# Weight rings kept across two stage borders, with the first two tiles split in the stage ahead

## The chip, the cores and the metric

The kernel runs on one core of a Trainium2 chip. Its engines are TensorE (PE; weight loads stand as PEld), VectorE (DVE), ScalarE (ACT), GpSimd (POOL) and SyncE (SP), which here only issues transfers. The metric is device time in microseconds of one execution; lower is better.

## The reference

Two layers of a diffusion backbone over 512 latent tokens and 256 context tokens of width 1024, all in float32. Each layer does, in this order for what matters here:

```python
P = _in_proj(h, w_in)                     # q, k, v, f, cs, co, gate: h @ w_in, column groups
cs = _token_shift(P['cs'], mu)            # inputs of the RWKV-7 branch
o_a = diff. attention(q, k, v)            # with 2-D rotary
o_f = real(fftn(f))                       # Fourier mixing over tokens and 128-wide groups
o_c = RWKV-7 scan in both directions      # state 64x64 per head, 8 heads
g = sigmoid(gate)
y = g0 * (o_a @ w_pa) + g1 * (o_f @ w_pf) + g2 * (o_c @ w_pc)
x = LN(alpha * x + gate1 * (y @ w_o))     # then a ConvGLU feed-forward sublayer of the same form
```

In the last layer only the latent tokens go through attention, the merges and the feed-forward part.

## The kernel before, in words

A layer is a row of stages. Each is a `with stage(nc)` block in which the five engines run their own instruction lists and meet through semaphores; at its end all engines meet, and the next stage begins with new semaphores. In order: `rwkv_inputs` (norm, then the projection of the `cs` and `co` columns, N = 15 tiles of 128 columns), `rwkv_scan`, `attention`, `merge_pa` (o_a @ w_pa, 8 tiles, with the RWKV output's group norm beside it), `close` (w_pc, w_pf, w_o and the Fourier transform), `ffn`.

**Weight tiles.** All big products are float32 made of three passes, (hi, hi), (hi, lo) and (lo, hi): each weight tile of 1024 x 128 is loaded into a ring `w_raw`, ACT copies it to the high part (`split_hi`, L324, counted by `w_hi`), and POOL subtracts that from the raw tile to get the low part (`split_lo`, L330, counted by `w_lo`). PE waits for `w_lo` before it uses a tile and counts `w_used` behind it. `weight_rings(sc, n_raw, n_split)` allocates the three rings. Before the change each stage allocates its own: 3 raw and 2 split buffers in `rwkv_inputs`, `rwkv_scan` and `close`, 2 and 2 in `merge_pa`. So the first tile of a stage is loaded and split after the stage has begun. `load_weights` (L313 to L316) makes SP wait until the buffer's last tile is split.

**The scan.** `rwkv_scan` works through six groups of 128 tokens, in both directions at once. Its many small matmuls wait for DVE and ACT, and PE fills these waits with the projection of the other `w_in` columns (v, f, gates, q, k): the `slots`, one weight tile each. `fill(point, g)` (L844 to L861) puts the next parts at named points of a group; `fill("first", 0)` runs the first 8 parts, tiles 0 and 1 and the latent half of tile 2, ahead of everything else. A tile has a piece of 512 latent tokens and one of 256 context tokens; the pieces use PSUM banks 6 and 7 in turn, so piece i waits at `result` for ACT's copy of piece i - 2 (L850, L1062). On ACT these copies stand in program order behind `decays(0, 0)` and `decays(0, 1)` (L1099, L1100), the exponentials (L1087 to L1097) of the cumulative sums that DVE makes in `sums` (L1148 to L1163); between the two, DVE does `scaled(0, 0)` (L1170 to L1184). `sums(0, d)` needs the inputs `sg`, `a`, `k`, `kk` of direction d, which SP loads in `inputs(0)` behind two mask tables and the load of tile 0; the rope table and tiles 1 and 2 follow. For tiles 0 and 1 POOL also makes the high part (L811), for later ones ACT does it once the copies of tile s - 2 are made (L1072 to L1081).

**The merge and `close`.** In `merge_pa` SP's loads are interleaved with `gate_in`, which waits for DVE's gated product (L1700) of tile j - 2. DVE's last product is the end of the stage, after PE's last tile. `close` starts with SP's loads of w_pc tiles 0 and 1 (512 rows, so half tiles of 256 KB), then the Fourier inputs `f`, the table `dft_w`, a gate and the big DFT tables. ACT copies the four parts of `oc` to `oc_hi` with the splits of the first two tiles between them (L1898, L1895), DVE makes `oc_lo` (L1993), PE multiplies tile 0 by k, and after every second k does one step of the transform (L1827), the first of which needs `f` and `dft_w`.

The lines the prediction speaks of:

```python
pe.wait_ge(sem("w_lo"), s + 1)                 # L848, the filler tile's low part
if i >= 2:
    pe.wait_ge(sem("result"), i - 1)           # L850, the bank of piece i - 2 is copied out
...
decays(0, 0)                                   # L1099, ACT, ahead of all copies
decays(0, 1)
copy_pieces(0, "first")
```

## Time and profile before

| | us |
|---|---|
| median of 3 runs | 3865.76 (3857.37 to 3866.92) |
| profiled execution: its own time | 3858.9 |
| its span | 3857.1 |
| mean granted TensorE clock | 0.957 |
| PE busy | 3435.0 (89%) |
| DVE, ACT, POOL busy | 1570.8 (41%), 1295.1 (34%), 1146.3 (30%) |
| DMA queue q1 | 413.55 MB, 33.9% of 16 engines |
| load of a w_in tile, 512 KB | 5.6 to landing, median |

Times in the trace count from the start of the span. The scan of layer 0 begins at 253.8, that of layer 1 at 2383.5; `close` begins at 1345.2 and 3283.6. "Idle before" in a row is how long the engine did nothing until that instruction, with what released it last. A granted clock of 1.00 is TensorE's upper level (2.4 GHz), 0.50 the lower one (1.2 GHz).

### The profile page before, as it was taken

The numbers are of one execution on the slowest core, as the hardware profiler recorded it, in microseconds if no ns is written. First come the engines' busy times: TensorE is split into PE (matmuls) and PEld (weight loads), VectorE is DVE, ScalarE is ACT, GpSimd is POOL, SyncE is SP. The second block draws the span as 40 slices with busy tenths as digits, with TensorE's granted clock in tenths as the row PEclk, the third lists the DMA queues.
The fourth block names the chain that finished last, engine by engine and source line by source line (L and its number), as shares of the span: only waits on it lengthen the run. The fifth ranks groups of instructions, "written<-read, shape, count | busy, mean of one in ns | idle before, by whom it ended". The sixth has DMA issues, their size and how long they took to land. (4 is left out here: it accounts for less than half of the span.)

```text
span 3857.1 us, 82372 instructions
## 1 busy us (share of the span) xinstructions
PE 3435.0 (89%) x36724; PEld 2751.4 (71%) x36724; DVE 1570.8 (41%) x2337; ACT 1295.1 (34%) x2096; POOL 1146.3 (30%) x677
## 2 busy tenths in 40 slices
PE   5979999999887899599999697999999897869997
PEld 3658888888655677487878465888878565558886
DVE  3243334432377544612121534344443375362224
ACT  3322233333255422321212243333433365233222
POOL 2111132233001512433323332213333104245554
PEclk9989999999998999799999898999999998989998
DMA  6653323442222342133332145333342214423332
GB/s 223 225 183 107 109 88 92 121 124 91 76 73 73 121 143 89 50 117 120 114 126 82 44 134 165 102 106 120 118 119 87 94 66 125 166 71 93 94 98 87
DMA packets 444250, 427.60 MB, mean 111 GB/s; under 512 B 15540, under 2 KB 369002, under 8 KB 436986
## 3 DMA queue, kind: packets, MB, share of 16 engines
q1 hardware_dynamic: 442314, 413.55, 33.9%
q10 hardware_dynamic: 1584, 8.78, 0.6%
q8 instruction: 290, 4.75, 0.5%
q14 instruction: 62, 0.51, 0.0%
HBM read 333.54 MB, written 88.74 MB: 109 GB/s over the span
## 5 line engine op out<-in xcount | busy, mean ns | idle before, releaser
L856 PE MATMUL ps<-I-280_h_hi,I-1958_w_hi 128*128 128x256 f32 (+1 forms) x832 | 299.4, 360 | 19.1 <-POOL I-1959_w_lo L330 19.0
L856 PE MATMUL ps<-I-281_h_lo,I-1958_w_hi 128*128 128x256 f32 (+1 forms) x832 | 283.3, 340 | 3.4 <-issue 3.4
L856 PE MATMUL ps<-I-280_h_hi,I-1959_w_lo 128*128 128x256 f32 (+1 forms) x832 | 283.1, 340 | 0.0
L2223 POOL TENSOR_TENSOR I-18452_w_lo<-I-18450_w_raw,I-18451_w_hi 128x1024 fp32r<-128x1024 f32 x65 | 156.9, 2414 | 374.6 <-ACT I-18451_w_hi L2182 374.5
L856 PE MATMUL ps<-I-23226_h_hi,I-24623_w_hi 128*128 128x512 f32 (+1 forms) x544 | 214.4, 394 | 17.4 <-POOL I-24624_w_lo L330 15.6
L2223 POOL TENSOR_TENSOR I-38403_w_lo<-I-38401_w_raw,I-38402_w_hi 128x1024 fp32r<-128x1024 f32 x65 | 156.3, 2405 | 168.3 <-ACT I-38402_w_hi L2182 168.3
L856 PE MATMUL ps<-I-23226_h_hi,I-24624_w_lo 128*128 128x512 f32 (+1 forms) x544 | 201.9, 371 | 0.0
L856 PE MATMUL ps<-I-23227_h_lo,I-24623_w_hi 128*128 128x512 f32 (+1 forms) x544 | 201.6, 371 | 0.0
L2182 ACT ACTIVATE I-18451_w_hi<-I-18450_w_raw 128x1024 fp32r<-128x1024 f32 x65 | 68.9, 1060 | 386.7 <-PE ps L339 236.4
L330 POOL TENSOR_TENSOR I-1959_w_lo<-I-1957_w_raw,I-1958_w_hi 128x1024 fp32r<-128x1024 f32 x36 | 88.4, 2455 | 334.3 <-ACT I-1958_w_hi L1080 334.1
L856 PEld LDWEIGHTS ps<-I-280_h_hi,I-1958_w_hi 128*128 128x128 f32 x832 | 157.9, 190 | 41.5 <-POOL I-1959_w_lo L330 19.9
L339 PE MATMUL ps<-I-18447_h_hi,I-18451_w_hi 128*128 128x512 f32 x704 | 185.2, 344 | 1.0 <-DVE I-18448_h_lo L381 1.0
L339 PE MATMUL ps<-I-18447_h_hi,I-18452_w_lo 128*128 128x512 f32 x704 | 181.5, 339 | 0.0
L339 PE MATMUL ps<-I-18448_h_lo,I-18451_w_hi 128*128 128x512 f32 x704 | 180.7, 338 | 0.0
L330 POOL TENSOR_TENSOR I-24624_w_lo<-I-24622_w_raw,I-24623_w_hi 128x1024 fp32r<-128x1024 f32 x36 | 90.3, 2508 | 283.4 <-ACT I-24623_w_hi L1080 283.2
L856 PEld LDWEIGHTS ps<-I-280_h_hi,I-1959_w_lo 128*128 128x128 f32 x832 | 158.1, 190 | 22.7 <-issue 3.8
L856 PEld LDWEIGHTS ps<-I-281_h_lo,I-1958_w_hi 128*128 128x128 f32 x832 | 158.4, 190 | 14.4
L1062 ACT ACTIVATE I-1960_result<-ps 128x512 f32<-128x512 f32 x104 | 51.2, 493 | 342.1 <-PE ps L856 342.0
L339 PE MATMUL ps<-I-38398_h_hi,I-38402_w_hi 128*128 128x512 f32 x352 | 137.6, 391 | 1.9 <-DVE I-38399_h_lo L381 1.9
L2182 ACT ACTIVATE I-38402_w_hi<-I-38401_w_raw 128x1024 fp32r<-128x1024 f32 x65 | 68.9, 1060 | 205.7 <-PE ps L339 119.6
L339 PE MATMUL ps<-I-38398_h_hi,I-38403_w_lo 128*128 128x512 f32 x352 | 136.9, 389 | 0.0
L339 PE MATMUL ps<-I-38399_h_lo,I-38402_w_hi 128*128 128x512 f32 x352 | 136.9, 389 | 0.0
(856 smaller groups left out, 8922.7 us busy)
## 6 DMA issues: line engine op xcount, KB each, us to landing
I-1957_w_raw<-in_w_in SPq DMA_DIRECT2D x52, 512.0 KB, 5.6
I-24622_w_raw<-in_w_in SPq DMA_DIRECT2D x52, 512.0 KB, 5.3
I-18460_ada_w<-in_ada_w SPq DMA_DIRECT2D x24, 1024.0 KB, 5.9
I-18450_w_raw<-in_ffn_up SPq DMA_DIRECT2D x44, 512.0 KB, 3.9
I-38401_w_raw<-in_ffn_up SPq DMA_DIRECT2D x44, 512.0 KB, 3.9
proj_d<-I-1960_result SPq DMA_DIRECT2D x52, 384.0 KB, 2.8
I-482_ada_w<-in_ada_w SPq DMA_DIRECT2D x16, 1024.0 KB, 5.7
I-18450_w_raw<-in_ffn_down SPq DMA_DIRECT2D x22, 512.0 KB, 3.3
```

Of the source, the lines that this page charges most:

```text
L330: eng.tensor_tensor(rings[2][:, n % n_split, 0:kt, :], rings[0][:, n % n_raw, 0:kt, :], rings[1][:, n % n_split, 0:kt, :].bitcast(F32), AL ...
L339: m = pe.matmul(dst[:, at:at + n], w[wi][:, k, :], a[ai][:, k, at:at + n], start=k == 0 and i == 0, stop=k == kt - 1 and i == 2)
L856: m = pe.matmul(bank(6 + i % 2, n_c), w[:, k, :], hv[:, k, c0:c0 + n_c], start=k == 0 and v == 0, stop=k == KT - 1 and v == 2)
L1062: act.activation(res[:, s % 2, c0:c0 + n_c], bank(6 + i % 2, n_c), ACT.Copy, scale=DH_A ** -0.5 if J_Q <= slots[s][0] < J_K else 1.0).then ...
L2182: act.activation(rings[1][:, g % 2, :, :], rings[0][:, g % 3, :, :], ACT.Copy).then_inc(sem("w_hi"), 1)
L2223: pool.tensor_tensor(rings[2][:, g % 2, :, :], rings[0][:, g % 3, :, :], rings[1][:, g % 2, :, :].bitcast(F32), ALU.subtract).then_inc(sem ...
```

## The change

The rings of `rwkv_inputs` and `rwkv_scan` become one set, allocated ahead of both, and so do those of `attention` (which only takes the argument), `merge_pa` and `close`, with 3 raw and 2 split buffers.

`rwkv_inputs` loads three more tiles at the end (numbers 15, 16 and 17 of its ring, which are slots 0, 1 and 2 of the scan) and splits the first two: ACT's split of tile 15 stands ahead of its work for main tile 14, that of tile 16 behind it. SP issues the three loads right after the loop, ahead of the last ada load and of the last stores, and waits for the third before the stage ends. The scan starts with slots 0 and 1 split and slot 2 loaded; its ring positions are shifted by 15 (`o_w`), and its semaphores count from slot 2 for `w_hi` and `w_lo` and from slot 3 for the loads. The loads of slots 0 to 2, POOL's copies and splits of slots 0 and 1, and ACT's wait for `w_lo` before it makes a high part are gone.

`merge_pa` loads the first two tiles of w_pc as its tiles 8 and 9 and splits both: tile 8 before ACT's sigmoid for j = 7, tile 9 as ACT's last instruction, since it needs the buffer of tile 7. POOL's splits stand around `out(3)`. `close` starts with its tile 2.

```diff
@@ -485,6 +484,9 @@
                     sp.dma_start(raw_d[:, R_G, 0:width(R_G)], gd[:, 0:width(R_G)]).then_inc(sem("raw_out"), 16)
                 if n >= 13:
                     store_lora(n - 9)
+            for n in range(N, N + 3):
+                c = OFF_V + (n - N) * P
+                load_weights(sp, sem, rings, n, src[:, :, c:c + P])
             if ada:
                 ada_load(sp, sem, ring, N, ada[N])
...
@@ -583,8 +586,7 @@
                     act.activation(inv[:, :], side[0:HC, :], ACT.Sqrt).then_inc(sem("norm"), 1)
 
             for n in range(N):
-                if n + 1 < N:
-                    split_hi(act, sem, rings, n + 1)
+                split_hi(act, sem, rings, n + 1)
                 beside(2 * n)
+            split_hi(act, sem, rings, N + 1)
...
-            for n in range(1, N):
+            for n in range(1, N + 2):
                 split_lo(pool, sem, rings, n)
...
-    rings = weight_rings(s2, 3, 2)
+    raw = lambda s: rings[0][:, (s + o_w) % 3]
+    hi, lo = (lambda s, i=i: rings[i][:, (s + o_w) % 2] for i in (1, 2))
...
-                load_weights(sp, sem, rings, s, w_src[:, :, c:c + P])
+                if s >= 5:
+                    sp.wait_ge(sem("w_lo"), s - 4)
+                sp.dma_start(raw(s), w_src[:, :, c:c + P]).then_inc(sem(f"w_in{s % 3}"), 16)
...
             sp.dma_start(masks[:, :, :], A["masks"]).then_inc(sem("const"), 16)
             sp.dma_start(lvm[:, :, :], A["lvmasks"]).then_inc(sem("const"), 16)
-            load(0)
             inputs(0)
             sp.dma_start(rope[:, :, :], A["rope"]).then_inc(sem("rope"), 16)
-            load(1)
-            load(2)
...
-                if s < 2:
-                    pool.wait_ge(sem(f"w_in{s % 3}"), 16 * (s // 3 + 1))
-                    pool.tensor_copy(rings[1][:, s % 2, :, :], rings[0][:, s % 3, :, :]).then_inc(sem("w_hi"), 1)
+                pool.wait_ge(sem("w_hi"), s - 1)
                 if s in turned:
...
-                    split_lo(pool, sem, rings, s)
+                    pool.tensor_tensor(lo(s), raw(s), hi(s).bitcast(F32), ALU.subtract).then_inc(sem("w_lo"), 1)
...
-            split(0)
-            split(1)
             for s in range(2, len(slots)):
                 pool.wait_ge(sem("piece"), ends[s - 2])
                 split(s)
...
                     if ks[0] == 0:
-                        pe.wait_ge(sem("w_lo"), s + 1)
+                        if s >= 2:
+                            pe.wait_ge(sem("w_lo"), s - 1)
                         if i >= 2:
                             pe.wait_ge(sem("result"), i - 1)
...
                             if i + 1 == ends[s] and s + 2 < len(slots):
-                                act.wait_ge(sem("w_lo"), s + 2)
-                                act.wait_ge(sem(f"w_in{(s + 2) % 3}"), 16 * ((s + 2) // 3 + 1))
-                                w_in, w_out = rings[0][:, (s + 2) % 3], rings[1][:, s % 2]
+                                if s >= 1:
+                                    act.wait_ge(sem(f"w_in{(s + 2) % 3}"), 16 * ((s + 2) // 3))
+                                w_in, w_out = raw(s + 2), hi(s + 2)
...
-        rings = weight_rings(sc, 2, 2)
...
+        after = A["w_pc"][l].rearrange("(k p) n -> p k n", p=P)
...
+            for j in range(2):
+                load_weights(sp, sem, rings, KT + j, after[:, :, j * P:(j + 1) * P])
...
             for j in range(KT):
-                if j + 1 < KT:
-                    split_hi(act, sem, rings, j + 1)
+                split_hi(act, sem, rings, j + 1, HA if j + 1 < KT else CTILES)
...
+            split_hi(act, sem, rings, KT + 1, CTILES)
...
+            split_lo(pool, sem, rings, KT, CTILES)
             out(3)
-
-def close(l, oc, y, last):
+            split_lo(pool, sem, rings, KT + 1, CTILES)
...
-        rings = weight_rings(s2, 3, 2)
+        raw = lambda n: rings[0][:, (n + KT) % 3]
+        hi, lo = (lambda n, i=i: rings[i][:, (n + KT) % 2] for i in (1, 2))
...
-                if n >= 3:
-                    sp.wait_ge(sem("w_lo"), n - 2)
+                if n >= 5:
+                    sp.wait_ge(sem("w_lo"), n - 4)
                 if n < M:
                     kind, j = slots[n]
-                    sp.dma_start(rings[0][:, n % 3, 0:CTILES, :], w_in[kind][:, :, j * P:(j + 1) * P]).then_inc(sem(f"w_in{n % 3}"), 16)
+                    sp.dma_start(raw(n)[:, 0:CTILES, :], w_in[kind][:, :, j * P:(j + 1) * P]).then_inc(sem(f"w_in{n % 3}"), 16)
...
-            weights(0)
-            weights(1)
             sp.dma_start(f[:, :, 0:n_tok], proj_d[J_F:J_F + F_GROUPS, :, 0:n_tok].rearrange("j p n -> p j n")).then_inc(sem("f"), 16)
             sp.dma_start(dw[:, :], A["dft_w"]).then_inc(sem("f"), 16)
             gate_in(0)
...
-                whi, wlo = slot(rings, n)
-                pe.wait_ge(sem("w_lo"), n + 1)
+                whi, wlo = hi(n), lo(n)
+                if n >= 2:
+                    pe.wait_ge(sem("w_lo"), n - 1)
...
-                act.wait_ge(sem(f"w_in{n % 3}"), 16 * (n // 3 + 1))
-                if n >= 2:
-                    act.wait_ge(sem("w_used"), n - 1)
-                act.activation(rings[1][:, n % 2, 0:kt_of(n), :], rings[0][:, n % 3, 0:kt_of(n), :], ACT.Copy).then_inc(sem("w_hi"), 1)
+                act.wait_ge(sem(f"w_in{n % 3}"), 16 * (n // 3 + (n % 3 == 2)))
+                act.wait_ge(sem("w_used"), n - 1)
+                act.activation(hi(n)[:, 0:kt_of(n), :], raw(n)[:, 0:kt_of(n), :], ACT.Copy).then_inc(sem("w_hi"), 1)
 
             for k in range(CTILES):
                 act.activation(ocp[0][:, k, :], oc[:, k, 0:n_tok], ACT.Copy).then_inc(sem("oc_hi"), 1)
-                if k < 2:
-                    split(k)
...
-            for n in range(N):
-                split_lo(pool, sem, rings, n, kt_of(n))
+            for n in range(2, N):
+                pool.wait_ge(sem("w_hi"), n - 1)
+                pool.tensor_tensor(lo(n)[:, 0:kt_of(n), :], raw(n)[:, 0:kt_of(n), :], hi(n)[:, 0:kt_of(n), :].bitcast(F32),
+                                   ALU.subtract).then_inc(sem("w_lo"), 1)
...
-            rwkv_inputs(l, h, last)
+            rings = weight_rings(s2, 3, 2)
+            n_w = rwkv_inputs(l, h, rings, last)
             with ExitStack() as s3:
-                rwkv_scan(l, s3, h, last)
+                rwkv_scan(l, s3, h, rings, n_w, last)
         oc = sb(sc, "oc", [P, CTILES, TOK])
         y = sb(sc, "y", [P, KT, TOK])
+        rings = weight_rings(sc, 3, 2)
         with ExitStack() as s2:
             oa = x[:, :, :].rearrange("p t d -> p (t d)").rearrange("p (j n) -> p j n", j=HA)
-            attention(l, oa, last)
-            merge_pa(l, oa, oc, y, last)
-        close(l, oc, y, last)
+            attention(l, oa, rings, last)
+            merge_pa(l, oa, oc, y, rings, last)
+        close(l, oc, y, rings, last)
```

## Rows read from the trace of the kernel before

**Rows 1.** The page's costliest groups: line, engine, shapes, count | busy, mean ns | idle before, releaser.

```profile
L856 PE MATMUL ps<-I-280_h_hi,I-1958_w_hi 128*128 128x256 f32 (+1 forms) x832 | 299.4, 360 | 19.1 <-POOL I-1959_w_lo L330 19.0
...
L330 POOL TENSOR_TENSOR I-1959_w_lo<-I-1957_w_raw,I-1958_w_hi 128x1024 fp32r<-128x1024 f32 x36 | 88.4, 2455 | 334.3 <-ACT I-1958_w_hi L1080 334.1
```

**Rows 2.** Timeline of PE, scan of layer 0: start us, us, engine, line [idle before].

```profile
264.77 0.79 PE L856 MATMUL ps<-I-280_h_hi,I-1958_w_hi 128*128 128x512 f32 x1 [15.45 <-POOL I-1959_w_lo L330]
...
275.50 0.28 PE L856 MATMUL ps<-I-280_h_hi,I-1959_w_lo 128*128 128x256 f32 x1
279.28 0.50 PE L856 MATMUL ps<-I-280_h_hi,I-1958_w_hi 128*128 128x512 f32 x1 [3.50 <-POOL I-1959_w_lo L330]
...
289.37 0.39 PE L856 MATMUL ps<-I-280_h_hi,I-1958_w_hi 128*128 128x512 f32 x1
```

**Rows 3.** Timeline of PE, scan of layer 1.

```profile
2394.58 0.80 PE L856 MATMUL ps<-I-23226_h_hi,I-24623_w_hi 128*128 128x512 f32 x1 [15.56 <-POOL I-24624_w_lo L330]
...
2407.49 0.47 PE L856 MATMUL ps<-I-23226_h_hi,I-24623_w_hi 128*128 128x512 f32 x1 [1.84 <-ACT I-24625_result L1062]
...
2415.91 0.28 PE L856 MATMUL ps<-I-23226_h_hi,I-24624_w_lo 128*128 128x256 f32 x1
```

**Rows 4.** Timeline of SP's queue, start of the scan, layer 0.

```profile
254.66 0.43 SPq L316 DMA_DIRECT2D I-1957_w_raw<-in_w_in  x1
```

**Rows 5.** Timelines of DVE, then POOL, then ACT, scan of layer 0.

```profile
261.36 1.23 DVE L1148 TENSOR_TENSOR_SCAN I-1943_L<-I-1914_reset,I-1931_sg 128x512 f32<-128x512 f32 x1 [6.74 <-DMA I-1931_sg<-sg_d]
262.62 2.65 DVE L1150 TENSOR_TENSOR I-1944_Lx<-I-1943_L,I-1931_sg 128x512 f32<-128x512 f32 x1
...
272.42 1.23 DVE L1148 TENSOR_TENSOR_SCAN I-1943_L<-I-1914_reset,I-1932_sg 128x512 f32<-128x512 f32 x1
...
261.55 3.17 POOL L330 TENSOR_TENSOR I-1959_w_lo<-I-1957_w_raw,I-1958_w_hi 128x1024 fp32r<-128x1024 f32 x1
...
275.01 0.63 ACT L1087 ACTIVATE I-1944_Lx<-I-1944_Lx 128x512 f32<-128x512 f32 x1 [6.58 <-DVE I-1934_Lr L1153]
...
277.56 0.87 ACT L1062 ACTIVATE I-1960_result<-ps 128x512 f32<-128x512 f32 x2
```

**Rows 6.** Timeline of DVE, scan of layer 1.

```profile
2392.42 2.65 DVE L1150 TENSOR_TENSOR I-24609_Lx<-I-24608_L,I-24596_sg 128x512 f32<-128x512 f32 x1
...
2402.76 1.53 DVE L1153 TENSOR_TENSOR I-24599_Lr<-I-24608_L 128x512 f32<-128x512 f32 x1
```

**Rows 7.** Timelines around merge and close, layer 0: DVE, SP, ACT, PE, POOL.

```profile
1343.37 0.95 DVE L1700 TENSOR_TENSOR I-13482_y<-I-16057_gate,ps 128x768 f32<-128x768 f32 x1 [7.36 <-PE ps L339]
...
1345.22 0.94 SPq L1785 DMA_DIRECT2D I-16885_w_raw<-in_w_pc  x2
...
1348.05 0.63 ACT L1895 ACTIVATE I-16886_w_hi<-I-16885_w_raw 128x512 fp32r<-128x512 f32 x1 [1.98 <-DMA I-16885_w_raw<-in_w_pc]
...
1350.09 1.01 PE L339 MATMUL ps<-I-16900_oc_hi,I-16886_w_hi 128*128 128x512 f32 x2 [6.76 <-POOL I-16887_w_lo L330]
...
1355.33 2.07 PE L1827 MATMUL ps<-I-16902_dft_w,I-49_x 128*128 128x256 f32 x4 [1.03 <-DMA I-16902_dft_w<-in_dft_w]
...
1360.98 1.29 POOL L330 TENSOR_TENSOR I-16887_w_lo<-I-16885_w_raw,I-16886_w_hi 128x512 fp32r<-128x512 f32 x1 [8.98 <-ACT I-16886_w_hi L1895]
```

**Rows 8.** Windows: stretch, length, busy (count) per engine, PE clock, DMA share, GB/s.

```profile
256.00:261.00 5.00, 0.00 (x0) 0.00 (x0) 0.00 (x0) 0.00 (x0) 0.57 (x1) 0.50 1.05 302
264.80:269.90 5.10, 5.10 (x12) 4.03 (x13) 4.96 (x9) 2.50 (x6) 0.00 (x0) 0.50 1.13 298
1346.50:1350.00 3.50, 0.00 (x0) 0.00 (x0) 1.12 (x2) 1.95 (x4) 1.24 (x1) 0.79 0.89 275
...
2376.00:2394.00 18.00, 2.90 (x4) 1.16 (x4) 4.36 (x5) 1.28 (x1) 4.23 (x3) 0.50 0.84 261
```

**Rows 9.** Timeline of DVE, end of the merge, layer 1.

```profile
3282.04 0.69 DVE L1700 TENSOR_TENSOR I-34669_y<-I-36620_gate,ps 128x512 f32<-128x512 f32 x1 [4.75 <-PE ps L339]
```

**Rows 10.** One line's instructions, L619: ns min/median/max, first and last start.

```profile
L619 DVE SCALAR_TENSOR_TENSOR I-283_k_and_kk<-I-283_k_and_kk,I-53_pa,ps x4: 1004/1010/1015, 230.2 to 249.4; 128x768 f32<-128x768 f32 x4
```

More of the change, by code:

```diff
@@ L419, in program, with rwkv_inputs @@
         LAT = ((0, SEQ),)
-        def rwkv_inputs(l, h, last):
+        def rwkv_inputs(l, h, rings, last):
             mains = (R_W, R_A, 0, 1, 2, 3, R_G, 10, 11, 12, 13, 4, 5, 6, 7)
@@ L503, in _ @@
                     sp.wait_ge(sem("kept"), 16)
+                    sp.wait_ge(sem(f"w_in{(N + 2) % 3}"), 16 * ((N + 2) // 3 + 1))
                 @block.tensor
@@ L648, in _, with rwkv_scan @@
                         ada_add(dve, sem, 1, 0, 2, 7)
-        def rwkv_scan(l, s2, h, last):
+            return N
+        def rwkv_scan(l, s2, h, rings, o_w, last):
             G = [P, GCOL]
@@ L808, in split @@
                     def split(s):
[L809 to L811 removed]
+                        pool.wait_ge(sem("w_hi"), s - 1)
                         if s in turned:
[L813 removed]
                             for v in range(2):
[L815 to L816 removed]
+                                m = pool.tensor_tensor(halves(lo(s))[:, :, v], paired(raw(s))[:, :, v],
+                                                       halves(hi(s))[:, :, v].bitcast(F32), ALU.subtract)
                             m.then_inc(sem("w_lo"), 1)
                         else:
[L819 removed]
+                            pool.tensor_tensor(lo(s), raw(s), hi(s).bitcast(F32), ALU.subtract).then_inc(sem("w_lo"), 1)
                     def rotate(s):
@@ L1276, in _, with attention @@
                                 dve.tensor_tensor(y, y, half(2 * d).rearrange("p i (t c) -> p t i c", t=CTILES), ALU.add).then_inc(sem("Ysum"), 1)
-        def attention(l, oa, last):
+        def attention(l, oa, rings, last):
             nq = LT if last else NT
@@ L1516, in _, with merge_pa @@
                             act.activation(oa[:, j, 0:q_tok], p_of(j), ACT.Copy, scale=subln[l][:, :]).then_inc(sem("oa"), 1)
-        def merge_pa(l, oa, oc, y, last):
+        def merge_pa(l, oa, oc, y, rings, last):
             seqs = LAT if last else BOTH
@@ L1728, in _, with close @@
                             out(j - 3)
+                    split_lo(pool, sem, rings, KT, CTILES)
                     out(3)
-        def close(l, oc, y, last):
+                    split_lo(pool, sem, rings, KT + 1, CTILES)
+        def close(l, oc, y, rings, last):
             seqs = LAT if last else BOTH
@@ L1780, in weights @@
                     def weights(n):
-                        if n >= 3:
-                            sp.wait_ge(sem("w_lo"), n - 2)
+                        if n >= 5:
+                            sp.wait_ge(sem("w_lo"), n - 4)
                         if n < M:
                             kind, j = slots[n]
-                            sp.dma_start(rings[0][:, n % 3, 0:CTILES, :], w_in[kind][:, :, j * P:(j + 1) * P]).then_inc(sem(f"w_in{n % 3}"), 16)
+                            sp.dma_start(raw(n)[:, 0:CTILES, :], w_in[kind][:, :, j * P:(j + 1) * P]).then_inc(sem(f"w_in{n % 3}"), 16)
                         else:
                             _, c, k = slots[n]
-                            sp.dma_start(wide(rings[0][:, n % 3]), w_o[:, 2 * k:2 * k + 2, c * 512:(c + 1) * 512]).then_inc(sem(f"w_in{n % 3}"), 16)
+                            sp.dma_start(wide(raw(n)), w_o[:, 2 * k:2 * k + 2, c * 512:(c + 1) * 512]).then_inc(sem(f"w_in{n % 3}"), 16)
                     def gate_in(n):
```

6 lines of the change are left out of this document (1 added, 5 removed).

## The prediction, made before the run

> **What bounds the kernel now.** I read the page's list of costly groups first. TensorE is busy for 89% of the span, and the group of L856 matmuls, the "filler" projection work of the scan, stood idle 19.1 us in layer 0, nearly all for POOL's low-half split (L330) [rows 1]. Then the PE timeline. In layer 0 the first L856 matmul starts at 264.77 after 15.45 us of idleness, its tile ends at 275.62 (last start plus one step of 0.12), and the second tile starts only at 279.28, after 3.50 us more [rows 2]. In layer 1 the first wait is 15.56 us, the second 1.84 us, and the second one ends on ACT's copy of a result, not on a weight [rows 3]. That row decides the case: the weights of the first two tiles are not the only thing at the start of the scan. Last I read what else runs there (DVE, ACT, POOL, the DMA queue) and the same for the start of `close`, where PE waits 6.76 us for a split and 1.03 us for a DFT table [rows 4 to 7].
>
> **Scan: what really releases the second tile.** After the change PE can run tile 0 at once, from about 253.9 (stage start, as SP's load is at 254.66 [rows 4], third in its queue). But tile 1 needs the PSUM bank of tile 0, which ACT frees (`result`), and ACT comes to that copy only after both `decays`. They hang on the DVE chain, and that on the `sg` input's DMA. In layer 0 the chain is: DVE scan at 261.36, second scan 272.42, ACT's first exponential for direction 1 at 275.01, copies at 277.56 [rows 5]. So of the 11 us that the first matmul starts earlier, nearly all turns into idleness between tile 0 and tile 1. What is won is what this chain gains:
> - The 512 KB tile leaves the queue ahead of `sg`. The stretch moves 302 GB/s [rows 8], so 524 KB are 1.74 us. I bound it by 0 (the queue's front was free anyway) and 3.5 us (512-byte rows at half that rate), and take the measured rate, since the queue is busy throughout.
> - POOL's cast and split of tiles 0 and 1 go. DVE's subtraction at 262.62 took 2.65 us beside POOL's 3.17 us split [rows 5]; a DVE operation over 512 elements otherwise takes 0.69 [rows 9]. That is 1.96 us, bounds 0 and 1.96.
> - The extra issues: SP drops one issue of 0.43 us ahead of the inputs [rows 4]; the queue is what lasts, so I count 0.
>
> Layer 0: 277.56 - 1.74 - 1.96 = 273.86, one copy of about 0.5 (half of 0.87 and the hand-over), PE at 274.36 instead of 279.28: 4.92 us. Layer 1 has the same two terms (2.65 us again) and a third, 1.53 instead of 0.69 on L1153 [rows 6]: 1.74 + 1.96 + 0.84 = 4.54 us against a start at 2407.49.
>
> **The clock takes part of it back.** A tile at the upper level (2.4 GHz) takes 2415.91 + 0.12 - 2407.49 = 8.54 us [rows 3]. After the long idle stretch tile 0 of layer 0 took 10.85 us [rows 2], 5.1 us of it at a granted clock of 0.50, the lower level of 1.2 GHz [rows 8]: a cold restart costs 2.31 us. Tile 1 of layer 0 took 289.37 - 279.28 = 10.09 us, so it already pays 1.55. With some 9 us of idleness ahead of it, tile 1 will pay 2.31 in both layers: 0.76 more in layer 0, and 2.31 more in layer 1, where it paid nothing after a gap of 1.84. Bounds: no fall at all (4.6 us better over both layers), or twice as long (4.6 worse). Net 4.2 and 2.2 us.
>
> **The tail of the input stage.** SP issues three loads of tiles 15 to 17, each waiting for `w_lo` of a tile split long before, ahead of the last ada load, the stores and the `kk` stores. The last of these waits ends before tile 14 is multiplied, and the ada block behind it is used only after tile 14; so 0, and if that cover went, up to one 512 KB transfer (1.74 us) in layer 0. ACT's two extra splits (about twice the 0.63 us of a half tile [rows 7]) and POOL's (2.455 us by its group [rows 1]) lie under tile 14 and under the normalisation that ends the stage on DVE and its store. The DVE operations of L619 there read PSUM; the four of layer 0 all take 1.00 to 1.02 us [rows 10]. If POOL's split stretched the third one as it stretches L1150, layer 1 would lose up to 1.96 us. I take 0: L1700, with a PSUM operand too, shows no stretch [rows 7, 9].
>
> **Merge, tail.** The second w_pc tile can be split only when tile 7 of w_pa is used up, which is the end of the stage. Before, DVE's last product (0.95 us, from 1343.37) closed it and the next stage's loads were issued at 1345.22 [rows 7]. Now ACT's copy of half a tile (0.63), a hand-over (an estimate: 0.08, as between rows of a chain) and POOL's 1.29 come to 2.00 us: 1.05 later. In layer 1 the product takes 0.69 [rows 9]: 1.31 later. The rest of the merge keeps its order: its loads are behind `gate_in`, which waits for PE's progress, so a third raw buffer buys nothing.
>
> **Close.** PE will start some 2 us after the stage start (ACT copy, DVE subtraction) instead of 4.9. But it meets the next wait after two k steps: the DFT step, released at 1355.33 by the DMA queue [rows 7]. That queue has the two w_pc tiles at its front, 524 KB at 275 GB/s: 1.91 us [rows 8]. Without them the table lands 1.91 earlier relative to the stage start, and the stage start is 1.05 or 1.31 later: 0.86 and 0.60 us. Bounds: all 1.91 kept in each layer, or nothing of it, which leaves a loss of 1.05 + 1.31. The later transfers shift alike.
>
> **Sum.** 4.2 + 2.2 + 0.9 + 0.6 = 7.9 us, 0.2%. The profiled execution took 3858.9 us (span 3857.1), so that one becomes 3851.0. The median of the runs shown, 3865.76, lies 6.9 above it, so I predict 3858.
>
> **A rule of the Trainium skill on the transfers.** The rows show 302 and 275 GB/s with weights in the mix [rows 8]. "DMA: Bandwidth & Descriptors", section "Anatomy of one DMA", prices a transfer at a fixed 2 us, mostly completion latency, plus bytes over 436 GB/s, so that a tile taken out of a busy queue gives back 1.2 us and not 1.74 or 1.91. By the page the sum would be 7.9 - 2 x 0.54 - 2 x 0.71 = 5.4 us. The trace does not agree with that rate in these stretches.
>
> **Rivals.**
> - Little is won (17%): the inputs' landing doesn't move, because the queue waits for something other than the tile ahead. For it: the masks stand ahead too. Against it: the DMA share in that stretch is 1.05 [rows 8]. The scan's terms lose 1.74 each, `close` becomes -1.05 and -1.31: 7.9 - 3.5 - 3.8 = 0.6 us, 3865.
> - More is won (20%): the clock recovers at once, or the rows of 512 bytes were the queue's slow part. 7.9 + 4.6 = 12.5 us, 3853; with twice the front's worth 19.8, 3846. Against it: the 5.1 us at 0.50 after such a gap [rows 8].
> - The whole wait goes (2%): PE never waits for the result copies. Then 11 us in each scan and 4.9 less 1.2 in each `close`: 29 us, 3836. Rows 3 speak against it.
> - Slower (5%): the clock stays low after the broken start. TensorE showed 0.50 over a whole sparse stretch of 18 us [rows 8]. Place: the scan from tile 1 on. Each microsecond at the lower level costs 0.5. Without any clock loss the sum is 4.92 + 1.55 + 4.54 + 0.86 + 0.60 = 12.5 us, so it decides at 12.5 us of low clock in each layer; with 30 us each (tiles 1, 2 and the first products) it costs 30 and the kernel is 17 us slower, 3883. Against it: tile 0 recovered within 5.1 us.
> - My forecast holds 56%, with an own range of 3853 to 3863.
>
> **Chances and range.** About 0.3% (11.6 us) is what a measurement of this kernel tells from no change. Faster by more: the whole-wait case, most of "more is won" and a tenth of my own case, 0.24. Slower: 0.05. The rest, 0.71, is no change. The runs before span 9.6 us, which widens the range: 3848 to 3867.
>
> **What would show it.** First L856 matmul within 1 us of the stage start and tile 0 at 10 to 11 us; then 8 to 10 us idle, put down to ACT L1062 in both layers, not to POOL L330; tile 1 at a clock of 0.50 for its first 3 to 6 us; L1150 at 0.69. POOL's L330 as the last instruction of the merge, and the DFT step of `close` still released by a DMA. It is wrong if the second tile starts without a wait, if the DFT step starts more than 2.5 us earlier relative to the last merge matmul, or if the input stage ends later than before.

## The result, and the profile after

The changed kernel takes 3837.61 us (median of 4 runs, 3834.83 to 3842.16), the kernel before 3864.88 beside it: ratio 0.9936, 95% interval 0.9924 to 0.9949. Measured again beside the experiments it took 3844.33 (5 runs) against 3859.34, ratio 0.9961 (0.9947 to 0.9974). By these ratios the change makes the kernel 15 to 25 us faster (the first two medians lie 27 apart), where 8 were forecast and "no change" got 0.71. The profiled execution has a span of 3836.4 us, 20.7 less than before.

The page's group of costly L856 matmuls, which stood 19.1 us idle for POOL in layer 0 [rows 1], now stands idle for ACT's copy of tile 0's result and for the stage's start. Each row gives busy time and mean ns, then the idle time in front and its largest releaser:

```profile
L856 PE MATMUL ps<-I-280_h_hi,I-283_w_hi 128*128 128x256 f32 (+1 forms) x832 | 298.5, 359 | 14.3 <-ACT I-1974_result L1062 9.8
...
L856 PE MATMUL ps<-I-23169_h_hi,I-23172_w_hi 128*128 128x512 f32 (+1 forms) x544 | 213.6, 393 | 12.4 <-ACT I-24582_result L1062 7.9
```

The timeline of PE at the scan's start, layer 0 and then layer 1 (it answers to [rows 2, 3]): tile 0's first and last matmul, tile 1's first, and the first products (L879), for which all the early tiles are only filler. "PEq" in a row is PE's own sequencer:

```profile
252.64 0.76 PE L856 MATMUL ps<-I-280_h_hi,I-283_w_hi 128*128 128x512 f32 x1 [4.53 <-PEq L123]
...
263.27 0.28 PE L856 MATMUL ps<-I-280_h_hi,I-284_w_lo 128*128 128x256 f32 x1
273.35 0.80 PE L856 MATMUL ps<-I-280_h_hi,I-283_w_hi 128*128 128x512 f32 x1 [9.80 <-ACT I-1974_result L1062]
...
289.55 0.70 PE L879 MATMUL ps<-I-1966_kk_in,I-1956_Bh 64*64 64x64 f32 x32
...
2369.74 0.77 PE L856 MATMUL ps<-I-23169_h_hi,I-23172_w_hi 128*128 128x512 f32 x1 [4.47 <-PEq L123]
...
2388.15 0.79 PE L856 MATMUL ps<-I-23169_h_hi,I-23172_w_hi 128*128 128x512 f32 x1 [7.89 <-ACT I-24582_result L1062]
...
2405.03 0.69 PE L879 MATMUL ps<-I-24574_kk_in,I-24564_Bh 64*64 64x64 f32 x32
```

The same for the kernel before, whose scans start at 253.81 and 2383.46 (the changed kernel's at 252.60 and 2369.70); the middle row belongs to the pace, below:

```profile
294.71 0.40 PE L856 MATMUL ps<-I-280_h_hi,I-1959_w_lo 128*128 128x512 f32 x1
295.04 0.69 PE L879 MATMUL ps<-I-1949_kk_in,I-1939_Bh 64*64 64x64 f32 x32
...
2421.70 0.69 PE L879 MATMUL ps<-I-24614_kk_in,I-24604_Bh 64*64 64x64 f32 x32
```

Tile 1 starts 20.75 us after the stage instead of 25.47, and the first products come at 36.95 instead of 41.23 us in layer 0 and at 35.33 instead of 38.24 in layer 1: 4.3 and 2.9 us won. Each is a number of one execution, and single ones move by a microsecond or two (scan_only, below).

The chain behind it, in the timelines of DVE and then ACT (it answers to [rows 5]):

```profile
258.46 1.22 DVE L1148 TENSOR_TENSOR_SCAN I-1960_L<-I-1931_reset,I-1948_sg 128x512 f32<-128x512 f32 x1 [5.06 <-DMA I-1948_sg<-sg_d]
259.72 0.69 DVE L1150 TENSOR_TENSOR I-1961_Lx<-I-1960_L,I-1948_sg 128x512 f32<-128x512 f32 x1
...
267.57 1.22 DVE L1148 TENSOR_TENSOR_SCAN I-1960_L<-I-1931_reset,I-1949_sg 128x512 f32<-128x512 f32 x1
...
270.15 0.63 ACT L1087 ACTIVATE I-1961_Lx<-I-1961_Lx 128x512 f32<-128x512 f32 x1 [6.56 <-DVE I-1951_Lr L1153]
...
272.70 0.87 ACT L1062 ACTIVATE I-1974_result<-ps 128x512 f32<-128x512 f32 x2
```

Merge and close of layer 0, timelines of DVE, ACT, POOL, SP and PE (answering to [rows 7]):

```profile
1335.34 0.95 DVE L1702 TENSOR_TENSOR I-13428_y<-I-16003_gate,ps 128x768 f32<-128x768 f32 x1 [7.36 <-PE ps L339]
1335.68 0.63 ACT L324 ACTIVATE I-13430_w_hi<-I-13429_w_raw 128x512 fp32r<-128x512 f32 x1 [7.23 <-PE ps L339]
1336.39 1.26 POOL L330 TENSOR_TENSOR I-13431_w_lo<-I-13429_w_raw,I-13430_w_hi 128x512 fp32r<-128x512 f32 x1 [5.50 <-ACT I-13430_w_hi L324]
1338.26 0.37 SPq L1801 DMA_DIRECT2D I-49_x<-proj_d  x1
1338.68 0.50 SPq L1802 DMA_DIRECT2D I-16859_dft_w<-in_dft_w  x1
...
1340.17 1.01 PE L339 MATMUL ps<-I-16857_oc_hi,I-13430_w_hi 128*128 128x512 f32 x2 [4.86 <-DVE I-16858_oc_lo L1996]
...
1345.10 1.13 PE L1830 MATMUL ps<-I-16859_dft_w,I-49_x 128*128 128x256 f32 x4 [1.28 <-DMA I-16859_dft_w<-in_dft_w]
```

The next stage's first DMA is issued 1.97 us after DVE's last product ends, before 0.90. The DFT step, still released by the DMA of `dft_w`, starts 6.82 us after close begins, before 10.10; in layer 1 5.50 instead of 8.93.

Windows of the scan's start (columns as in [rows 8]): the two stretches at the lower clock around tile 1, and the queue ahead of the `sg` input.

```profile
268.00:278.00 10.00, 4.65 (x11) 3.69 (x12) 9.83 (x12) 4.31 (x9) 2.82 (x1) 0.50 0.49 141
2384.20:2394.20 10.00, 6.05 (x14) 4.79 (x15) 5.84 (x10) 4.20 (x9) 2.94 (x1) 0.50 0.43 124
...
256.00:261.00 5.00, 5.00 (x22) 4.06 (x22) 2.50 (x4) 0.00 (x0) 0.00 (x0) 0.84 1.08 292
```

All that doesn't add up to 20.7 us. A stage's time can be divided into three: PE's idle time, PE's busy time with the part at the lower clock counted half ("the rest" from here on), and the other half of that part, which is what the lower clock costs. One term is explained by no wait and no clock: the rest of the scans fell from 719.7 to 716.2 and from 599.7 to 595.9 us. It is the pace of the 512-column matmuls. Here the first and the last of 24 in a row, in the timeline of PE after; before, such a run went from 289.37 [rows 2] to the 294.71 shown above:

```profile
283.99 0.40 PE L856 MATMUL ps<-I-280_h_hi,I-283_w_hi 128*128 128x512 f32 x1
...
289.23 0.39 PE L856 MATMUL ps<-I-280_h_hi,I-284_w_lo 128*128 128x512 f32 x1
```

23 steps take 5.34 us before and 5.24 after: 232.2 and 227.8 ns. Over about a thousand such steps of a scan at full clock, the mean is 232.1 before and 228.8 after; the 256-column ones go the other way, 118.6 to 119.2.

### The profile page after: what moved, and what is told of

It reads as the page before. It is cut to its first block and busy times, and to the rows that moved or that the text cites. A ratio compares the mean times of both kernels' runs of the same rounds, so it can differ in the third digit from the quotient of the medians.

```text
span 3836.4 us, 82276 instructions
## 1 busy us (share of the span) xinstructions
PE 3431.1 (89%) x36724; PEld 2754.2 (72%) x36724; DVE 1552.4 (40%) x2337; ACT 1298.0 (34%) x2100; POOL 1139.2 (30%) x673
## 5 line engine op out<-in xcount | busy, mean ns | idle before, releaser
L856 PE MATMUL ps<-I-280_h_hi,I-283_w_hi 128*128 128x256 f32 (+1 forms) x832 | 298.5, 359 | 14.3 <-ACT I-1974_result L1062 9.8
L856 PE MATMUL ps<-I-280_h_hi,I-284_w_lo 128*128 128x256 f32 (+1 forms) x832 | 282.7, 340 | 3.0 <-issue 3.0
L856 PE MATMUL ps<-I-281_h_lo,I-283_w_hi 128*128 128x256 f32 (+1 forms) x832 | 283.1, 340 | 0.0
L856 PE MATMUL ps<-I-23169_h_hi,I-23172_w_hi 128*128 128x512 f32 (+1 forms) x544 | 213.6, 393 | 12.4 <-ACT I-24582_result L1062 7.9
L856 PE MATMUL ps<-I-23170_h_lo,I-23172_w_hi 128*128 128x512 f32 (+1 forms) x544 | 201.8, 371 | 0.8 <-issue 0.8
L856 PE MATMUL ps<-I-23169_h_hi,I-23173_w_lo 128*128 128x512 f32 (+1 forms) x544 | 201.6, 371 | 0.0
L856 PEld LDWEIGHTS ps<-I-280_h_hi,I-283_w_hi 128*128 128x128 f32 x832 | 159.0, 191 | 39.2 <-ACT I-1974_result L1062 10.0
L339 PE MATMUL ps<-I-18390_h_hi,I-18394_w_hi 128*128 128x512 f32 x704 | 184.1, 343 | 1.7 <-DVE I-18391_h_lo L381 1.7
L339 PE MATMUL ps<-I-18390_h_hi,I-18395_w_lo 128*128 128x512 f32 x704 | 181.8, 339 | 0.0
L339 PE MATMUL ps<-I-18391_h_lo,I-18394_w_hi 128*128 128x512 f32 x704 | 180.8, 338 | 0.0
L856 PEld LDWEIGHTS ps<-I-280_h_hi,I-284_w_lo 128*128 128x128 f32 x832 | 159.1, 191 | 17.5
L856 PEld LDWEIGHTS ps<-I-281_h_lo,I-283_w_hi 128*128 128x128 f32 x832 | 159.5, 192 | 14.1
L339 PE MATMUL ps<-I-38284_h_hi,I-38288_w_hi 128*128 128x512 f32 x352 | 138.4, 393 | 1.9 <-DVE I-38285_h_lo L381 1.9
L339 PE MATMUL ps<-I-38285_h_lo,I-38288_w_hi 128*128 128x512 f32 x352 | 137.8, 391 | 0.0
L339 PE MATMUL ps<-I-38284_h_hi,I-38289_w_lo 128*128 128x512 f32 x352 | 137.7, 391 | 0.0
```

What stands on the lines that cost most here:

```text
L339: m = pe.matmul(dst[:, at:at + n], w[wi][:, k, :], a[ai][:, k, at:at + n], start=k == 0 and i == 0, stop=k == kt - 1 and i == 2)
L856: m = pe.matmul(bank(6 + i % 2, n_c), w[:, k, :], hv[:, k, c0:c0 + n_c], start=k == 0 and v == 0, stop=k == KT - 1 and v == 2)
```

## The experiments

**Which part brings it.** Four kernels, measured together with the kernel before (3855.84 us there).

place: of the change only where the rings are allocated.

```
-    rings = weight_rings(s2, 3, 2)       # in rwkv_scan, rwkv_inputs, close, merge_pa
+    rings = weight_rings(s2, 3, 2)       # once around inputs and scan, once around merge and close
```

> The kernel before with nothing changed but where the weight rings lie in SBUF: they are allocated in the outer scopes of the change, every load and split stays where it was. Placement theory: the filler matmuls of the scan (L856) start 226 to 228 ns apart at full clock instead of 229 to 233, as in the changed kernel, and the two scans get 3.5 us shorter each, so the whole is 5 to 8 us faster than before. Stage-start theory (the gain is all in waits at the stage starts and in the clock): within 2 us of before, pace of the matmuls as before.

Measured 3853.61 us, ratio 0.9981 (0.9968 to 0.9993), which is 7 us; the two medians lie only 2.2 apart. The rest of the scans is 716.4 and 595.95 us and the pace 228.8 ns, so no load or split, but the place of tiles makes the matmuls faster. By the rest of the two scans that is worth 7.2 us. The first products of layer 0 come at 41.3 us as before, but those of layer 1 at 42.1 instead of 38.2: tile 1 waited 4.04 us there for ACT's copy (1.84 before), and PE's clock was at 0.83 in the 10 us behind it. What made that wait longer is not known.

scan_only: the rings kept, loads and splits ahead of the scan; merge and close as before.

> The first half of the change: rings shared by the input stage and the scan, three loads and two splits ahead; merge and close as before. Stage-start theory: 2 x 4.7 us at the second filler tile, less about 3 us of clock, 6 to 7 us in all. With the placement theory on top: 12 to 15 us, and the rest of the gain of 25 us then has to be in the other half.

Measured 3843.55, ratio 0.9958 (0.9944 to 0.9972). That is 16 us, a little above the 12 to 15 expected with the pace. The first products come at 34.9 us in both layers, the DFT step at 9.7 and 9.1 us. The scan is the same as in the changed kernel, which had 36.95 and 35.33: so much differs between single executions.

close_only: the other half; inputs and scan as before.

> The second half of the change: rings shared by merge and close, w_pc tiles 0 and 1 loaded and split in the merge; inputs and scan as before. If the two w_pc tiles at the queue's front are worth 3.3 to 3.4 us each time, as the traces of before and after show, and the merge ends 1.07 us later, 4.6 us in all; with the prediction's 1.91 it would be 1.5 us. Anything over 6 us is a change of clock or of pace elsewhere.

Measured 3854.15, ratio 0.9993 (0.9984 to 1.0002), by itself no difference that the runs can tell, though 4.6 us, as expected, lie inside the interval. The trace has the effect: the DFT step comes 6.6 us after close's first DMA (SP and PE in the timeline), and 5.6 in layer 1; the scan's pace is 232.0.

```profile
1346.51 0.37 SPq L1801 DMA_DIRECT2D I-49_x<-proj_d  x1
...
1353.13 0.80 PE L1830 MATMUL ps<-I-16913_dft_w,I-49_x 128*128 128x256 f32 x1 [0.50 <-DMA I-16913_dft_w<-in_dft_w]
```

loads_only: the changed kernel, but POOL casts and splits tiles 0 and 1 in the scan, from data that is already there.

```
+    for s in range(2):
+        pool.tensor_copy(hi(s), raw(s)).then_inc(sem("h01"), 1)
+        pool.wait_ge(sem("h01"), s + 1)
+        pool.tensor_tensor(lo(s), raw(s), hi(s).bitcast(F32), ALU.subtract).then_inc(sem("l01"), 1)
```

> The changed kernel, but the scan's first two tiles are only loaded in the input stage; POOL makes their high and low parts at the start of the scan, as before. Tells the queue from POOL: if the queue's front alone is 1.74 us and POOL's port the other 1.96, the chain that frees the bank of tile 0 ends about 2 us later than in the changed kernel in each layer, 3 to 4 us slower than it in all. If DVE is not slowed by POOL but was by the queue, no difference to the changed kernel.

Measured 3844.13, ratio 0.9967 (0.9954 to 0.9979). First products at 37.9 and 36.3 us, each 1.0 later than with the splits ahead, so by this trace the loads bring most of what the scan's start wins. POOL's work has not become harmless for DVE, though. It lies earlier and meets DVE's first scan instead of the subtraction behind it (timelines of DVE, then POOL):

```profile
258.74 3.44 DVE L1156 TENSOR_TENSOR_SCAN I-1950_L<-I-1921_reset,I-1938_sg 128x512 f32<-128x512 f32 x1 [4.19 <-DMA I-1938_sg<-sg_d]
262.22 0.69 DVE L1158 TENSOR_TENSOR I-1951_Lx<-I-1950_L,I-1938_sg 128x512 f32<-128x512 f32 x1
...
258.73 2.37 POOL L840 TENSOR_TENSOR I-284_w_lo<-I-282_w_raw,I-283_w_hi 128x1024 fp32r<-128x1024 f32 x1
```

That scan takes 3.44 and, in layer 1, 2.54 us instead of 1.23, and ACT's copies come 1.35 and 2.2 us later than in the changed kernel.

**The wait that is left.** after_again repeats the changed kernel; copy_early lets ACT copy tile 0's results between the two decay groups:

```
     decays(0, 0)
+    copy_parts(parts[0:3])          # the two pieces of tile 0
     decays(0, 1)
-    copy_pieces(0, "first")
+    copy_parts(parts[3:n_first])
```

> The changed kernel once more, beside the others of this job. Theory P (placement of the weight tiles plus shorter fronts): 3836 to 3846 us, 16 to 20 us under the kernel before, split as the parts run alone showed it: scan part about -16, close part about -3. The 512-column L856 matmuls again start 228.8 ns apart at full clock (the kernel before: 232.1), the DFT step of close starts 6.8 us (layer 0) and 5.5 us (layer 1) after close begins. Rival (the first measurement's 27 us was real and the parts multiply): 3829 us or 27 us under the kernel before of this job.

> The changed kernel, but ScalarE copies the two finished pieces of weight tile 0 between the two decay groups of the scan's first group and not behind both. Theory (the idle time left at the scan's start is the wait for that copy): the second tile's matmuls start near 264.4 us instead of 273.35 in layer 0 and near 2381 instead of 2388.15 in layer 1, the 10 us at half clock behind the wait go as well, and nothing later takes the time back, since the VectorE chain of d=1 is done 13 us before PE asks for it: -14 to -23 us against the changed kernel, most likely -18. Rival (the wait moves on: tile 2's first piece waits for the copy behind the second decay group, and the VectorE operands of the first products): -3 to -8 us. Rival (the low clock comes anyway at the next short wait): -14 at most.

after_again: 3844.33, ratio 0.9961; the DFT step at 6.87 and 5.55 us, pace 228.8. copy_early: 3825.63 (3818.93 to 3829.54), ratio 0.9913 (0.9899 to 0.9926), 18.7 us under the changed kernel. The timeline of PE, then a window of the same columns as above:

```profile
264.79 0.50 PE L856 MATMUL ps<-I-280_h_hi,I-283_w_hi 128*128 128x512 f32 x1 [1.28 <-ACT I-1974_result L1065]
...
276.05 0.47 PE L856 MATMUL ps<-I-280_h_hi,I-283_w_hi 128*128 128x512 f32 x1 [2.65 <-ACT I-1974_result L1065]
...
281.66 0.69 PE L879 MATMUL ps<-I-1966_kk_in,I-1956_Bh 64*64 64x64 f32 x32
```

```profile
265.00:275.00 10.00, 8.40 (x48) 7.23 (x47) 9.70 (x12) 3.04 (x8) 2.83 (x1) 1.00 0.80 240
276.00:286.00 10.00, 8.65 (x212) 7.33 (x215) 7.97 (x10) 1.72 (x3) 2.98 (x1) 1.00 0.33 95
```

The 9.80 us of idleness are 1.28 (ahead of tile 1) and 2.65 (ahead of tile 2) now, in layer 1 1.02 and 1.27 instead of 7.89, and the clock is at its upper level where it was at 0.50. The first products come at 29.15 and 26.87 us, 7.8 and 8.5 sooner: 16.3 of the 18.7 us. The theory's 18 us came; the first rival had seen the second wait (2.65 us), but not how little it costs, and the third, 14 us at most, is exceeded.

**What the front of close's queue costs.** front512 puts 524 KB in 512-byte rows back ahead of the spectrum loads; front_wide the same bytes in rows of 2 KB.

```
+    for d in range(2):
+        sp.dma_start(raw(3 + d)[:, 0:CTILES, :], w_in["pf"][:, :, (2 + d) * P:(3 + d) * P])
     sp.dma_start(f[:, :, 0:n_tok], proj_d[J_F:J_F + F_GROUPS, ...])
```

> The changed kernel with two loads of 256 KB in 512-byte rows put back in front of the close stage's first spectrum loads; their data is used by nothing, the destination is waited for later. Theory Q (each KB at the front of the queue in 512-byte rows costs as it did in the kernel before): the DFT step starts 10.1 +-0.4 us after close begins (6.8 in the changed kernel), the layer 1 one 8.9 (5.5). Rival (it was the splits and not the loads at the front that made it late): it stays at 6.8 and 5.5. By my 1.91 us for 524 KB: 8.7 and 7.4.

> As the kernel with two 256 KB loads ahead, but each partition's 2 KB lie in one stretch of DRAM and not in four rows of 512 bytes. If the size of the rows sets the cost: the DFT step starts 8.2 to 8.7 us after close begins in layer 0 (1.4 to 1.9 us later than in the changed kernel) and 6.9 to 7.4 in layer 1. If bytes alone set it: 10.1 and 8.9, as with the 512-byte rows.

One execution each. The timelines of front512, then of front_wide (SP's first issue and the DFT step, layer 0):

```profile
1342.52 0.92 SPq L1804 DMA_DIRECT2D I-13429_w_raw<-in_w_pf  x2
...
1353.60 0.80 PE L1834 MATMUL ps<-I-16859_dft_w,I-49_x 128*128 128x256 f32 x1 [5.26 <-DMA I-16859_dft_w<-in_dft_w]
```

```profile
1345.32 0.81 SPq L1804 DMA_DIRECT2D I-13429_w_raw<-in_dft_lat  x2
...
1355.01 0.79 PE L1834 MATMUL ps<-I-16859_dft_w,I-49_x 128*128 128x256 f32 x1 [3.86 <-DMA I-16859_dft_w<-in_dft_w]
```

The step comes at 11.06 and 8.87 us with 512-byte rows (4.24 and 3.37 later than in the changed kernel), at 9.67 and 9.30 with wide ones (2.85 and 3.80 later). So the loads at the front make the step late, and not the splits: 524 KB cost 2.9 to 4.2 us either way, not 1.91. A difference by the size of the rows doesn't show. Nor could a small one: in the nine profiled kernels that start close as before, the step comes at 9.4 to 11.1 us in layer 0 and at 8.3 to 9.6 in layer 1, on the mean at 10.07 and 9.03; in the nine that start it like the changed kernel, at 6.6 to 7.1 and 5.5 to 5.7, on the mean at 6.80 and 5.59. The difference of the means is 3.3 and 3.4 us.

**What about the place sets the pace.** Nine kernels; of each the start of the `w_hi` ring in bytes of a partition, its remainder by 256 (that of `h_hi` and `h_lo` is 192), and the mean step of L856's 512-column matmuls in the scan of layer 0. after_turned and after_pad are variants of the changed kernel, all others the kernel before with allocations moved, one execution profiled of each.

```
kernel         w_hi ring   mod 256   step
before          199,488       64    232.1 ns
rings_mid       170,816       64    232.0      rings ahead of L
tiles_turned    199,488       64    232.0      k_in to y_out ahead of W1T
place           108,992      192    228.8
rings_first     108,992      192    228.9      rings first in the scan's list
rings_low       121,536      192    228.9      rings behind S
rings_pad       199,616      192    228.8      + pad = sb(s2, "pad", [P, 32]) ahead of the rings
after_turned    108,992      192    228.8      the changed kernel, k_in to y_out ahead of W1T
after_pad       109,120       64    232.0      the changed kernel, + the same pad ahead of the rings
```

> The kernel before, with one line moved: in the scan's list of tiles the weight rings are allocated ahead of L and not behind y_out, so that they lie 28 KB lower per partition (raw at 158,528, hi at 170,816, lo at 179,008 bytes) and only the twelve 2 KB tiles L to y_out lie 28 KB higher. If the place of the rings themselves sets the pace of the 512-column L856 matmuls, it changes from 232.1 ns (to 228.8 if lower is better). If it is the place of the scan's work tiles (which the changed kernel moved too): those below L have not moved, the pace stays at 232, or goes a part of the way.

> The kernel before, with the rings where they were (raw 187,200, hi 199,488, lo 207,680 bytes) and the ten tiles k_in to y_out allocated ahead of W1T and not behind Lx, so that W1T to Lx lie 20 KB higher. If the place of the rings alone sets the pace of L856: 232.1 ns as before. If the place of the work tiles that VectorE, ScalarE and GpSimd write beside it sets it: some other pace between 228 and 236 ns.

> The kernel before, with the scan's rings allocated first of the scan's tiles (raw 96,704, hi 108,992, lo 117,184 bytes), where the changed kernel has them; the input stage and everything else as before. Theory (where the scan's own rings lie is the cause, not what the stages ahead did): L856's 512-column matmuls start 228.8 ns apart, and the input stage's stay as before. Rival (the shared allocation did something else): 232.1.

> The kernel before, with the scan's rings behind S (raw 109,248, hi 121,536, lo 129,728 bytes: low, but 192 past a multiple of 512 where h is 448 past one). If it is enough that the rings lie low, next to h (theory L): near 229. If their distance from h within 512 bytes counts (theory O: 448 and 448 in the changed kernel, 320 against 448 before): not 228.8, rather 232.

> The kernel before with an unused tile of 128 bytes ahead of the scan's rings: they stay high (raw 187,328, hi 199,616, lo 207,808) but are now 448 past a multiple of 512, as h is. Theory O: 228.8 ns. Theory L: 232.1 ns.

> The changed kernel, its rings in place (raw 96,704), with k_in to y_out allocated ahead of W1T. If only the rings' place sets the pace (L or O): 228.8 ns. If the other tiles' place takes part: another number.

Moving the rings by 28 KB (rings_mid) or other tiles by 20 KB (tiles_turned, after_turned) does nothing. 128 bytes do it. A run of 24 in rings_pad, then in after_pad (timelines of PE), 5.24 and 5.34 us:

```profile
289.03 0.40 PE L857 MATMUL ps<-I-280_h_hi,I-1959_w_hi 128*128 128x512 f32 x1
...
294.27 0.39 PE L857 MATMUL ps<-I-280_h_hi,I-1960_w_lo 128*128 128x512 f32 x1
```

```profile
282.88 0.39 PE L856 MATMUL ps<-I-280_h_hi,I-284_w_hi 128*128 128x512 f32 x1
...
288.22 0.40 PE L856 MATMUL ps<-I-280_h_hi,I-285_w_lo 128*128 128x512 f32 x1
```

rings_low refutes both theories as they were put: low and at 192 past a multiple of 512, it is fast. The remainder by 512 is not what counts, that by 256 fits all nine. Three things stay open, since no kernel varied them: only two remainders occur, 64 and 192; the three rings always moved together; and `h` never moved, so the rings' own place and their distance from `h` can't be told apart.

The pace also shows in the whole execution. The rest, summed over the twelve large stages, is 3354.5 to 3356.2 us in before, close_only, rings_mid and tiles_turned, and 3345.5 to 3347.9 in the fourteen profiled executions with the scan's rings at 192 (all but ffn_pad, below).

**Timed.** Four kernels, measured together with the kernel before (3860.99 us there).

> The kernel before with the unused 128-byte tile ahead of the scan's rings and nothing else. The traces so far: 512-column L856 matmuls 228.8 or 228.9 ns apart wherever the rings begin 192 bytes past a multiple of 256 (as h does), 232.0 to 232.4 where they begin 64 past one. If that is the whole of what the allocation brings: 7 us less than the kernel before (3.6 in each scan), ratio about 0.998. If the pace is a matter of the profiled execution alone: no change.

> The changed kernel with an unused 128-byte tile ahead of the rings that the input stage and the scan share, so that they begin 64 bytes past a multiple of 256 again. If the offset sets the pace: L856 at 232 ns, about 7 us slower than the changed kernel, so 8 to 10 us faster than the kernel before where the changed kernel is 15 faster, and the input stage's 512-column matmuls (L339) 3 ns faster than in the changed kernel. Rival (the 28 KB move is what counts): 228.8 ns and no change.

> The changed kernel with tile 0's early copy, and an unused 128-byte tile ahead of the ffn stage's rings, whose 512-column L339 matmuls start 234 to 237 ns apart in layer 0 in every kernel so far. If being off h's offset is bad everywhere, as in the scan: slower than with the early copy alone, by up to 5 us. If it helps there, as the input stage's rows hint (230 ns at 64 past, 234 at 192 past): up to 5 us faster. No effect: same.

> The changed kernel with tile 0's early copy, measured again on this chip beside the others: 31 to 35 us under the kernel before (ratio 0.991 to 0.992), so 16 to 20 under the changed kernel.

- pad_timed (the kernel before and 128 unused bytes): 3855.98 us, ratio 0.9982 (0.9970 to 0.9994), the same as place: 7 us by the ratio, 5.0 between the medians.
- after_pad: 3844.43, ratio 0.9948 (0.9930 to 0.9967). The pace went back to 232.0, the rest of the scans to 719.0 and 598.5 us and that of the whole execution to 3352.2, but the time shows no loss: 16 to 20 us under the kernel before, where 8 to 10 were expected. The interval is 14 us wide and the changed kernel was not measured beside it: 7 us is not decided here, only not confirmed.
- ffn_pad (copy_early with the pad ahead of the ffn's rings): 3832.65 (0.9922, 0.9905 to 0.9938) against 3827.28 (0.9905) for copy_early_again, intervals that overlap; the traces say more. In layer 0 the 512-column L339 steps get shorter (235 to 230.5 ns), the 256-column ones beside them longer (116.3 to 120.4), and the stage's rest stays (589.7 and 589.5 us). Layer 1 has only 512-column ones; they get longer, 226.8 to 233.0, and the stage 6.6 us longer. PE busy in that stage, windows of copy_early_again, then of ffn_pad:

```profile
3439.40:3821.90 382.50, 360.37 (x1578) 0.98 0.29 92
```

```profile
3437.30:3826.40 389.10, 367.00 (x1578) 0.98 0.29 91
```

copy_early is the fastest kernel measured. Its repetition, copy_early_again, is 33.7 us under the kernel before, 0.9905 (0.9885 to 0.9925), as in the first measurement.

## Why the prediction was wrong

It failed in two terms of its sum: the new place of the rings was priced at nothing, and what the two loads cost at the front of `close` was priced at 1.91 us and measured 3.3 and 3.4. The rest of its mechanism came as described, and so did its signs, two of them at the edge: in layer 1 the wait was 7.89 us where 8 to 10 were named, and the lower clock had 6.2 us of tile 1 where 3 to 6 were. The DFT step came 2.2 and 2.4 us earlier relative to the last merge matmul, under the 2.5 that would have refuted it. By its own steps:

- **Scan, what releases the second tile.** Right, in layer 0 also the size. PE does tile 0 at once and then waits 9.80 and 7.89 us for ACT's copies. The `sg` input's DVE scan starts 5.86 us after the stage instead of 7.55: 1.69 us for 1.74 forecast. L1150 takes 0.69 instead of 2.65. Tile 1 comes 4.72 us sooner (4.92 forecast) and in layer 1 5.58 (4.54); there the scan of `sg` came 2.68 us sooner instead of 1.74. That 1.69 came so close to 1.74 is luck in part. The scan of `sg` starts 7.1 to 8.4 us after the stage in the nine profiled kernels that load tile 0 ahead of it and 4.6 to 7.6 in the other eleven, and SP's issue ahead of it, counted as 0, is gone too. The Trainium skill's rule on a DMA's time ("DMA: Bandwidth & Descriptors", "Anatomy of one DMA"), stated for DMAs that GpSimd issues, gave an estimate of 1.2 us for this term; the traces don't fit it better: 1.69 and 2.68. POOL's share of 1.96 us is right too: the first DVE scan to the second takes 9.11 us instead of 11.06.
- **The clock takes part of it back.** Right. PEclk is 0.50 from 268 to 278, of which tile 1 has 4.7 us, and tile 1 takes 0.55 us longer than before in layer 0 and 2.8 in layer 1, forecast 0.76 and 2.31. Net, up to the first products, 4.3 and 2.9 us, forecast 4.2 and 2.2. The rival "the whole wait goes" is refuted in the changed kernel. Its price of 11 us per scan was about right: in copy_early, which takes nearly all of the wait away, the first products come 12.1 and 11.4 us sooner than in the kernel before.
- **Input stage.** Right: from its first load to the next stage 210.5 us before and 210.8 after in layer 0, 172.1 and 171.4 in layer 1.
- **Merge, tail.** Right: 1.07 us later (1.05 forecast), in layer 1 1.06 (1.31 forecast).
- **Close.** The mechanism was right, the term mis-sized: the step "524 KB at 275 GB/s: 1.91 us" measured 3.27 and 3.43. SP's own issues were left out: the spectrum load's issue (L1798) stood 0.97 us behind the first one (1345.22 [rows 7]) and is the first now. 1.91 + 0.97 make 2.9, if the two add; the other 0.4 to 0.5 were not taken apart. The timeline of SP before:

```profile
1346.19 0.51 SPq L1798 DMA_DIRECT2D I-49_x<-proj_d  x1
```

- **Sum.** Scan starts 7.2, fronts of close 6.7, merge tails -2.1: 11.8 us, where 7.9 were forecast. The failed step is what the sum doesn't have: the change part "rings allocated in an outer scope" was priced at nothing, and it changed the pace of the scans' L856 matmuls: 2,496 of 512 columns gain 3.2 us per thousand (8.0) and 1,632 of 256 columns lose 0.6 (1.0), by the stages' rest 3.5 and 3.7 us. With it 19.0 us. That this comes near the 20.7 between the profiled executions is luck, for the clock went the other way. Divided as above, over the twelve large stages of both layers:

| us | before | after |
|---|---|---|
| PE idle | 381.0 | 364.2 |
| the rest | 3356.2 | 3347.9 |
| cost of the lower clock | 53.2 | 59.6 |
| small stages and ends | 66.7 | 64.8 |

So idleness and the rest give 25.1 us. The terms above name 22.1 of them, when the scan starts are taken as the 4.72 and 5.58 us before the clock's loss; 3.0 were not taken apart. The clock took 6.4 back over the whole execution: close of layer 0 had 10.8 us less of busy time at the lower level (5.4 won), the attention stages 8.8 and 8.9 more (8.8 lost), ffn 4.7 and 3.1 more (3.9 lost).

- **The clock between executions.** The longer low stretch in attention is not shown to come from the change. In layer 0 it is 7.2 us in before, place, loads_only, copy_early and ffn_pad, and 9.3 to 16.2 in the other fifteen, of which six are the kernel before with allocations moved. One kernel has both: copy_early 7.2, copy_early_again 13.4, and over the large stages 110.8 and 128.7 us at the lower level. That difference costs 9.0 us, and their spans differ by 8.6. after and after_again have 119.1 and 130.6 us, which costs 5.8, and differ by 7.7. What sets the length of these stretches is open.
- **"Little won", "more won", "slower".** None came as it was told. "More won" had seen that the front could be worth more, up to twice, which `close` bears out (3.3 and 3.4 for 1.91), but neither of its reasons holds: the clock did not recover at once, and wide rows cost about as much as rows of 512 bytes. The range ended at 3848; 3837.61 and 3844.33 are below it. The kernel before itself has medians of 3855.84 to 3864.88 us in the four sets of runs, so a time forecast to the microsecond from one of them is off by several us before any term is wrong.

## What to carry to other kernels

When a producer is moved ahead, look for the next thing that the consumer needs, here the PSUM bank behind two groups of exponentials. Moving the copies that free it brought as much again as the whole change, 18.7 us against 15.0. An edit that only changes where tiles lie is not free of effect: read the step between matmuls at full clock in both traces before looking for a wait. And before a difference between two executions is explained, compare their busy time at the lower clock: here it alone made 9 us between two executions of one kernel.
